# Hybrid decoder step on one core: the LayerNorm shift as extra token columns, the last expert's transposes inside the preceding down projection, and two groups of loads moved

## What is computed

```python
def layer_norm(x, g, b):
    mu = x.mean(-1, keepdims=True)
    var = jnp.square(x - mu).mean(-1, keepdims=True)
    return (x - mu) * lax.rsqrt(var + LN_EPS) * g + b

def moe(x, ...):                       # w_gate, w_up (16,1024,512), w_down (16,512,1024)
    for e in range(N_EXPERTS):
        h = jax.nn.silu(xt @ w_gate[e]) * (xt @ w_up[e])
        y = y + combine[:, e:e + 1] * (h @ w_down[e])

def rglru_mixer(x, conv_hist, h0, w_in, conv_w, conv_b, ...):   # layer 1
    y_br, x_br = jnp.split(x @ w_in, 2, axis=-1)                # w_in (1024, 2048)
    y_br = jax.nn.gelu(y_br, approximate=True)
    xc, conv_new = causal_conv(x_br, conv_hist, conv_w, conv_b)
    ...                                                         # gates, scan, output projection

x = layer_norm(ALPHA * x + f, ln_ffn_g[0], ln_ffn_b[0])          # end of layer 0, feeds layer 1
```

## Time and profile before

| | |
|---|---|
| median of three runs | 1479.97 us |
| profiled execution | 1482.55 us, of which the span in the profile is 1480.8 us |
| PE busy | 1265.6 us (85%) |
| DVE busy | 980.4 us (66%) |
| ACT busy | 721.2 us (49%) |
| POOL busy | 205.6 us (14%) |
| mean granted TensorE clock | 0.899 of full |
| last down projection of layer 0 ends | 811.1 us after the span's start |
| first projection of layer 1 starts | 864.1 us |
| `c_w_out` is issued; the output projection that needs it starts | 969.1 us; 1040.0 us |
| last down projection of layer 1 ends | 1437.0 us |

### The profile page before, as it was taken

One profiled execution on the slowest core, in us unless ns is written; L12 is line 12 of the kernel. 1 busy time (PEld: TensorE's weight loads), 2 busy tenths in 40 slices (PEclk: granted clock), 3 DMA queues, 4 the chain that ended last, 5 costly groups with the idle time before them and its releaser, 6 DMA issues.

```text
span 1480.8 us, 18030 instructions
## 1 busy us (share of the span) xinstructions
PE 1265.6 (85%) x6469; PEld 1015.8 (69%) x6469; DVE 980.4 (66%) x1462; ACT 721.2 (49%) x988; POOL 205.6 (14%) x265
## 2 busy tenths in 40 slices
PE   4999978888899489999998279987994899999970
PEld 4989877776345378888886179953453788888850
DVE  2766345442334589999995543738445999999957
ACT  2533222212001288888884542255012888888843
POOL 3111342211200110000000200136001100000002
PEclk9999989987599599999999579998995999999995
DMA  6121060001332579999982912020425799999825
GB/s 194 58 66 49 1 211 1 1 1 50 111 145 100 206 279 410 409 415 408 421 351 100 312 47 86 1 114 0 174 107 199 289 398 419 414 412 415 345 100 191
DMA packets 63103, 296.60 MB, mean 200 GB/s; under 512 B 6625, under 2 KB 32970, under 8 KB 50753
## 3 DMA queue, kind: packets, MB, share of 16 engines
q1 hardware_dynamic: 51136, 252.78, 44.2%
q0 software_dynamic: 7296, 26.22, 4.8%
q10 hardware_dynamic: 4608, 16.78, 2.9%
HBM read 268.87 MB, written 26.89 MB: 200 GB/s over the span
## 4 chain that ended last, share of the span: by engine, by line
PE 79%; DVE 10%; ACT 4%; issue 3%; POOL 2%; DMA 1%; SPq 0%; POOLq 0%; DVEq 0%; ACTq 0%
PE bank L1026 24%; PE bank L1056 12%; PE bank L950 6%; PE bank L612 4%; PE bank L613 4%; PE bank L640 4%; PE bank L641 4%; PE bank L937 3%; PE bank L1016 2%; PE bank L1152 2%; PE bank L961 1%; PE bank L599 1%; PE bank L1044 1%; PE bank L836 1%; PE bank L701 1%
## 5 line engine op out<-in xcount | busy, mean ns | idle before, releaser
L1178 ACT ACTIVATE GU_HIGH<-work 128x1024 fp32r<-128x1024 f32 x256 | 269.8, 1060 | 65.0 <-PE bank L1026 65.0
L1026 PE MATMUL bank<-GU_HIGH,XGT_HIGH 128*128 128x512 f32 x512 | 206.1, 402 | 13.3 <-DVE XGT_LOW_B L2084 13.3
L2108 DVE TENSOR_TENSOR WUP_LOW<-work,GU_HIGH 128x1024 fp32r<-128x1024 f32 x128 | 153.5, 1221 | 15.9 <-ACT GU_HIGH L1178 11.6
L2108 DVE TENSOR_TENSOR WGT_LOW<-work,GU_HIGH 128x1024 fp32r<-128x1024 f32 x128 | 155.3, 1222 | 12.0 <-ACT GU_HIGH L1178 4.0
L2115 DVE TENSOR_TENSOR WDN_LOW<-work,WDN_HIGH 128x1024 fp32r<-128x1024 f32 x128 | 151.7, 1221 | 7.8 <-ACT WDN_HIGH L1178 3.6
L1178 ACT ACTIVATE WDN_HIGH<-work 128x1024 fp32r<-128x1024 f32 x128 | 135.3, 1063 | 43.6 <-PE bank L1056 43.6
L1178 ACT ACTIVATE work<-bank 128x512 f32<-128x512 f32 (+4 forms) x148 | 59.5, 445 | 134.1 <-PE bank L694 29.5
L1026 PEld LDWEIGHTS bank<-GU_HIGH,XGT_HIGH 128*128 128x128 f32 x512 | 98.5, 192 | 34.0 <-DVE XGT_LOW_B L2084 14.5
L1178 ACT ACTIVATE W_HIGH<-work 128x1024 fp32r<-128x1024 f32 x36 | 38.0, 1059 | 150.2 <-PE bank L613 80.6
L1056 PE MATMUL bank<-WDN_HIGH,HT_HIGH 128*128 128x512 f32 x256 | 103.9, 406 | 2.8 <-DVE HT_LOW L2095 2.8
L1026 PE MATMUL bank<-GU_HIGH,XGT_LOW_A 128*128 128x512 f32 x256 | 102.8, 402 | 0.0
(11 more groups left out here) (457 smaller groups left out, 2924.1 us busy)
## 6 DMA issues: line engine op xcount, KB each, us to landing
work<-in_moe_w_gate_dram SPq DMA_DIRECT2D x32, 2048.0 KB
work<-in_moe_w_up_dram SPq DMA_DIRECT2D x32, 2048.0 KB, 10.0
work<-in_moe_w_down_dram SPq DMA_DIRECT2D x32, 2048.0 KB, 9.4
y_rows<-work ACTq DMA_DIRECT2D x32, 512.0 KB, 10.3
work<-in_ab_w_in_dram SPq DMA_DIRECT2D x10, 1024.0 KB, 5.6
work<-in_c_w_in_dram SPq DMA_DIRECT2D x8, 1024.0 KB, 9.1
x_rows<-X SPq DMA_DIRECT2D x8, 512.0 KB, 2.6
work<-in_c_w_out_dram SPq DMA_DIRECT2D x1, 4096.0 KB, 12.8
```

The source lines that it names most:

```text
L1026: last = mm(psum, x, w, start=(k == m == 0), stop=(k == KD - 1 and m == 2))
L1178: return nc.scalar.activation(out, in_, ACT.Copy, scale=scale)
L2108: V.tensor_tensor(low[u][:, 2 * n:2 * n + 2, :], w[u][:, 2 * n:2 * n + 2, :], high, ALU.subtract)\
```

## The change

- `last_downs` puts the four transposes of expert 15 between slices 1 and 2 of down(14), into bank 4. Their high and low parts go to `XGT_HIGH` and `XGT_LOW_A`, whose tokens are no longer needed. down(15) accumulates in banks 0 and 2 in place of 7 and 6. Both layers do this.
- In `norm(1)` the transposed tile is only multiplied by the gain; the bias is not added. The bias column becomes two extra token columns (the same column twice) of `XT_HIGH` and `XT_LOW`, now 578 columns wide. The matmuls of the second token half have 290 columns. Column 288 of each result is the weight matrix times the bias; ACT copies it to `in_shift[:, c]` and adds it as the bias of the Gelu, or of an Identity in place of a copy.
- `mixer1_rows` now also makes the two columns' high and low parts, takes a Sqrt of a constant on ACT, and rounds and splits the weight blocks 0 and 1; `norm(1)` no longer does.
- SP loads the first two blocks of `c_w_in` after down(14), ahead of the wait for down(15); before, they came after the gate matrices. The tables of layer 1's first norm are loaded after the projections, ahead of `c_w_out`.

```diff
+            def down_part(u, g, f, high, low, banks):
+                pe.wait_ge(down_split, 4 * g + (f + 1))
+                for half in (1, 0):
+                    cols = slice(512 * half, 512 * half + 512)
+                    for n, (x, w) in enumerate(((high, WDN_HIGH), (high, WDN_LOW[u]), (low, WDN_HIGH))):
+                        last = mm(bank[banks[half]][:, :], x[:, f, :], w[:, f, cols],
+                                  start=(f == n == 0), stop=(f == 3 and n == 2))
+                last.then_inc(down_used, 1)
+            def last_downs(g):
+                pe.wait_ge(ht_ready, g)
+                pe.wait_ge(y1_out, g - 1)
+                for f in (0, 1):
+                    down_part(0, g - 1, f, HT_HIGH, HT_LOW, (7, 6))
+                pe.wait_ge(h_ready, g + 1)
+                for f in range(4):
+                    last = tr(heads_of(4)[:, f, :], every(HB[1], FF // P, f), ident[:, :])
+                last.then_inc(h_ps, 1)
+                for f in (2, 3):
+                    down_part(0, g - 1, f, HT_HIGH, HT_LOW, (7, 6))
+                pe.wait_ge(ht_ready, g + 1)
+                for f in range(4):
+                    down_part(1, g, f, XGT_HIGH, XGT_LOW_A, (0, 2))
...
                 up(l, 8, 1, base + 15)
-                down(l, 0, base + 14)
-                h_transposed(1, base + 15)
-                down(l, 1, base + 15)
+                last_downs(base + 15)
...
+                if l == 0:
+                    sp.wait_ge(down_used, 4 * (base + NE - 1))
+                    for n in range(2):
+                        sp.dma_start(W0[n], c_w_in[0].rearrange("(k p) c -> p k c", p=P)[:, :, 256 * n:256 * n + 256])\
+                          .then_inc(w_in[n], 16)
                 sp.wait_ge(down_used, 4 * (base + NE))
...
-                lnp(0, 1, ln_mix_g, ln_mix_b)
                 sp.wait_ge(ysel_in[2], 32)
...
-                for n in range(8):
+                for n in range(2, 8):
...
                 sp.wait_ge(proj_ps, NPROJ + 16)
+                lnp(0, 1, ln_mix_g, ln_mix_b)
                 sp.dma_start(WO1, c_w_out[0].rearrange("(k p) d -> p k d", p=P)).then_inc(wo_in, 16)
...
-                        last = mm(bank[(3, 6, 7)[c % 3]][:, 0:TH], w[:, k, :], x[:, k, TH:T], **ends)
+                        last = mm(bank[(3, 6, 7)[c % 3]][:, 0:TH + 2], w[:, k, :], x[:, k, TH:T + 2], **ends)
...
-                            last = nc.scalar.activation(XT[:, k, tile_cols(t)], heads_of(TILE_BANK(t) + 1, P, ROWS[t])[:, k - 4, :],
-                                                        ACT.Identity, bias=ffn_col[:, 1, k:k + 1], scale=ffn_col[:, 0, k:k + 1])
+                            last = copy(XT[:, k, tile_cols(t)], heads_of(TILE_BANK(t) + 1, P, ROWS[t])[:, k - 4, :],
+                                        ffn_col[:, 0, k:k + 1])
...
-                        for k in range(4):
-                            last = V.tensor_scalar(XT[:, k, tile_cols(t)], heads_of(TILE_BANK(t), P, ROWS[t])[:, k, :],
-                                                   ffn_col[:, 0, k:k + 1], ffn_col[:, 1, k:k + 1], ALU.mult, ALU.add)
-                        last.then_inc(xt_lo, 1)
+                        V.tensor_tensor(XT[:, 0:4, tile_cols(t)], heads_of(TILE_BANK(t), P, ROWS[t]),
+                                        ffn_col[:, 0, 0:4].unsqueeze(2).broadcast_to([P, 4, ROWS[t]]), ALU.mult).then_inc(xt_lo, 1)
...
+                g = base + 15
+                round_units("up", 8, 1, g)
+                store(1, g - 2, 13)
+                h_rounded(g - 1)
+                silu(1, g)
+                round_down(8, 1, g, (0, 1))
+                act.wait_ge(h_ps, g + 1)
+                copy(XGT_HIGH[:, 0:4, :], heads_of(4)).then_inc(ht_high, 1)
+                round_down(8, 1, g, (2, 3))
+                result(8, 0, g - 1)
+                store(0, g - 1, 14)
+                result(8, 1, g, 0)
+                store(1, g, 15)
...
+                act.wait_ge(hist_out, 3 + 3)
+                rounded.end(copy(XT_HIGH[:, :, T:T + 2], ffn_col[:, 1, :].unsqueeze(2).broadcast_to([P, KD, 2])), 0, "b")
+                nc.scalar.activation(norm_eps[:, 1:2], norm_eps[:, 0:1], ACT.Sqrt)
+                round_w(0)
+                round_w(1)
...
+                    shift = in_shift[:, c:c + 1]
+                    copy(shift, sbk[:, TH:TH + 1]).then_inc(shift_out, 1)
+                    act.wait_ge(shift_out, c + 1)
...
+                        for to, part in ((buf[:, CONV - 1:CONV - 1 + TH], pb[:, 0:TH]), (buf[:, CONV - 1 + TH:EXT_P], sbk[:, 0:TP - TH]),
+                                         (ext_samples(buf)[:, :, CONV - 1:], sbk[:, TP - TH:TH].rearrange("p (s l) -> p s l", s=NS))):
+                            last = nc.scalar.activation(to, part, ACT.Identity, bias=shift)
...
+                split_units("up", 1, g)
+                h_split(g - 1)
+                h_product(1, g)
+                split_down(1, g, (0, 1))
+                dve.wait_ge(ht_high, g + 1)
+                V.tensor_tensor(XGT_LOW_A[:, :, :], heads_of(4), XGT_HIGH[:, 0:4, :].bitcast(F32), ALU.subtract).then_inc(ht_ready, 1)
+                split_down(1, g, (2, 3))
+                result(8, 0, g - 1)
+                result(8, 1, g, 2)
...
+                rounded.wait(dve, 0, "b")
+                dve.wait_ge(y_stored[0], arrivals(0, 8))
+                split.end(V.tensor_tensor(XT_LOW[:, :, T:T + 2], ffn_col[:, 1, :].unsqueeze(2).broadcast_to([P, KD, 2]),
+                                          XT_HIGH[:, :, T:T + 2].bitcast(F32), ALU.subtract), 0, "b")
+                split_w(0)
+                split_w(1)
```

More of the change, by code:

```diff
@@ L220, in hybrid_trunk @@
         GI = view(26112, (KD, T))
-        EXT1 = [work[:, 30720 + EXT * s:30720 + EXT * (s + 1)] for s in range(3)]
-        TMP = view(32529, (2, T))
+        EXT1 = [work[:, 30752 + EXT * s:30752 + EXT * (s + 1)] for s in range(3)]
+        TMP = view(32561, (2, T))
         lhistT = view(33681, (KD, 24))
@@ L1051, in down @@
                 for f in range(4):
-                    pe.wait_ge(down_split, 4 * g + (f + 1))
-                    for half in (1, 0):
-                        cols = slice(512 * half, 512 * half + 512)
-                        for n, (x, w) in enumerate(((HT_HIGH, WDN_HIGH), (HT_HIGH, WDN_LOW[u]), (HT_LOW, WDN_HIGH))):
-                            last = mm(bank[7 - half][:, :], x[:, f, :], w[:, f, cols],
-                                      start=(f == n == 0), stop=(f == 3 and n == 2))
-                    last.then_inc(down_used, 1)
+                    down_part(u, g, f, HT_HIGH, HT_LOW, (7, 6))
+            def last_downs(g):
[12 more added lines that the diff above has]
+                    down_part(1, g, f, XGT_HIGH, XGT_LOW_A, (0, 2))
             def experts(l):
@@ L1368, in root @@
                         act.wait_ge(norm_stats, q * NT + t + 1)
-                        nc.scalar.activation(lnw[0:r, t, 14:15], lnw[0:r, t, 13:14], ACT.Sqrt, bias=norm_eps[0:r, :],
+                        nc.scalar.activation(lnw[0:r, t, 14:15], lnw[0:r, t, 13:14], ACT.Sqrt, bias=norm_eps[0:r, 0:1],
                                              scale=1.0 / D).then_inc(norm_root, 1)
@@ L1391, in norm @@
                 root(0)
-                for t in range(NT + 3):
+                for t in range(NT + 2):
                     if t + 1 < NT:
@@ L1454, in store, with step @@
                        .then_inc(y_stored[u], 16)
-                def step(i, v, before, more=True):
+                def step(i, v, before):
                     u, g = (1 + v) % 2, i * 2 + (base + 1 + v)
@@ L2109, in split_units, with split_down @@
                             .then_inc(gu_split, 1)
-                def split_down(u, g):
-                    for f in range(4):
+                def split_down(u, g, some=range(4)):
+                    for f in some:
                         dve.wait_ge(down_rounded, 4 * g + (f + 1))
```

80 lines of the change are left out of this document (31 added, 49 removed).

## The result

The changed kernel takes 1472.43 us at the median of four runs (1470.24 to 1473.53), the kernel before 1480.11 in four runs beside it (1479.16 to 1480.52). The ratio is 0.9947, with a 95% interval of 0.993 to 0.9964: 7.7 us less. The profiled execution took 1473.53, with a span of 1471.6 against 1480.8 before; its mean granted clock is 0.905 against 0.899.

The account below looks back on a forecast made before the run. PE was taken as the bound (79% of the chain). Terms -6.2 + 2.9 - 3.15 + 0.3 + 0.5 - 3.5 = -9.15 us gave 1470.8 from the 1479.97 median, put at 1471.0; range 1466.5 to 1476.

Parts of the forecast that it names:

- the tail in one piece at full clock: Sign: down(14), transposes and down(15) as one PE run of 11.4 to 11.8 us at full clock, both layers.
- the first sum behind block 1's split: Sign in layer 0's norm: DVE's first sum right behind the split of weight block 1, not behind a gather.
- 6.4 us a projection: Sign: projections take 6.4 us each as before; one longer than 6.5 us would be wrong.
- the gates 1.4 us after the last: Sign: PE starts the gates about 1.4 us after the last projection.
- The tails: End of the experts: closing PE's gap between down(14) and down(15) gives -6.2 us in layer 0, -3.5 in layer 1.
- Between the experts and the sums: Layer 0: new ACT and DVE work on bias columns, Sqrt and two weight blocks delays the first sum, +2.9 us.
- The table load: Early Sqrt's load, 1.28 us plus 0.2, counted ahead of layer 0's sums; its removal from the norm given nothing.
- The norm: Layer 0, first sum to first projection: one DVE step, shorter activations and no block 0 at the end, -3.15 us.
- The columns: Projections: 384 matmuls of the second token half have two more columns, +0.3 us at 2.4 GHz.
- the last eviction: ACT's extra column copy and bias pointers, hidden in all projections but the last before the gates, +0.5 us.
- rival 3: Projections: wider token arrays read more slowly; 12 ns more per matmul cancels the gain; 1490 or above, chance 0.06.
- Rival 2: Layer 0: weight block loads hold up expert 15's store, so the sums start 3.4 us later; 1474.4, chance 0.15.

Follow-up runs that it names:

- the tails alone: Kernel before with only the new order of the last two down projections; norm, bias and all loads as before: 1469.71 us, ratio 0.9931.
- the rest alone: Changed kernel's edits except the tails, with down(14), transposes and down(15) in the old order: 1481.91 us, ratio 1.0015 against the kernel before.
- The kernel without the early load: Changed kernel without the Sqrt of a constant ahead of the weight blocks, so its table load falls back into the norm: 1470.96 us, ratio 0.9942.
- the tails with the pitch: Tails alone, but with the two token arrays 578 columns apart per k slice in place of 576: 1471.8 us, ratio 0.9945.
- the load late: Changed kernel with the first two weight blocks loaded after expert 15's store has landed, preparation still ahead of the sums: 1471.91 us, ratio 0.9944.
- the kernel with the preparation in the loop: Changed kernel with rounding and splitting of weight blocks 0 and 1 moved into the norm's loop, early loads kept: 1471.38 us, ratio 0.9944.

## Why the prediction was right, and where it was not

1471.0 was forecast, 1472.43 measured, 1.4 us above it. All signs that the prediction named came out: the tail in one piece at full clock, the first sum behind block 1's split, 36 us of norm, 6.4 us a projection, the gates 1.4 us after the last.

**The tails: right in mechanism and size.** -6.2 was forecast for layer 0 and -6.35 measured, -3.5 and -3.6 for layer 1. Down(14), transposes and down(15) take 11.45 us in a piece; I had 11.57 with an allowance of 0.2 for late operands, of which nothing shows. The experiment with the tails alone gives the whole gain. Restarting down(15) cost 0.3 us in layer 1 (5.76 against 5.45), which the two numbers include.

**Half of the tail's gain in layer 0 is clock, and there the forecast had luck.** I took 3 us of half level as fixed for layer 0 and absent for layer 1, because one profile showed it so. The profile of the rest alone shows it in both layers with the same code, so layer 1 could have gained 2.5 us more. No profile shows layer 0 without it. The timed 9.6 us of the tails alone (8.4 to 12.1 by the interval) fits one fall in the kernel before, as an average; none would give about 6.9 and two about 12.5, an estimate from the segments.

**Between the experts and the sums: the step was right, the size was off.** +2.9 forecast, +3.6 measured. DVE's first sum stands behind block 1 and not behind a gather, as the prediction said. The work itself took a little less: the first sum starts 2.6 us later than with the tails alone when the small loads are undisturbed (16.54 against 13.98). The term that was missing is the issue and landing of the nine small loads behind two 1 MB blocks, 1.0 us. I had written that they "move with it"; what moves past a queue's other work has to be costed again.

**The table load: I gave its removal from the norm nothing, which holds.** The kernel without the early load has a norm 0.16 us longer, hardly more than one profile can tell. Ahead of the sums it costs 1.6 us, of which I had counted 1.5. The Trainium skill's 2.66 us for a switch of tables ("ScalarE: Activation LUTs", section "What ACT_TABLE_LOAD costs") is not what this case shows: the load at 815.71 takes 1.28 and the next root follows it by 0.01 us, and taking load and root away gives 1.6 us in all.

**The norm: -3.15 forecast, -3.5 measured.** All kernels with the norm's part show 35.6 to 36.9 us against 38.9 to 39.1. No run splits this into its three edits, but the two timelines place the terms. The four activations of tile 0 to `XT`, before and in the changed kernel:

```profile
836.56 1.48 ACT L1189 ACTIVATE XT<-bank,ffn_col 128x128 f32<-128x128 f32 x4
```

```profile
831.70 1.12 ACT L1202 ACTIVATE XT<-bank,ffn_col 128x128 f32<-128x128 f32 x4
```

They take 0.36 us less where I had 0.3. DVE's step takes 0.69 in place of 1.37, and from tile 0's step to tile 1's it is 3.65 us in place of 4.33: -0.68, as forecast (-0.7), once. The three later steps each follow 0.36 sooner, and the short tile's four activations take 0.37 less: -1.46 together, forecast -1.15. The end, without block 0, gives -1.2 (-1.3), and 0.2 comes ahead of tile 0's step, which I had not counted.

**The columns and the last eviction.** Eviction +0.5 forecast, +0.47 measured. The matmuls +0.3 forecast, +0.67 measured: +1.0 at the full clock for the pitch against before, -0.3 because the clock rose three matmuls earlier. The columns themselves, the term that I had priced, cost next to nothing. The miss is rival 3 in small. I had said that it needs 12 ns a matmul to turn the result; it is 1.0 to 1.3.

**The layer 1 stretches.** I forecast nothing for the 452 us between the first gate and the last experts. The changed kernel took 0.9 more there, the others with the norm's part 0.3 to 1.4 more, the tails alone 0.4 less, the tails with the pitch 0.75 more. The changed kernel's repetition shows 0.9 again, so scatter between executions is not the likely cause. In all eleven profiles with the kernel's normal flow the difference arises in the first 205 us; over the rest, in layer 1's experts, they agree within 0.02 us. Nothing in that stretch was tested; its cause is open.

**Rival 2** had the mechanism right, its size too large and the consequence wrong. The store of expert 15 is held up by the weight blocks: it takes 6.11 us to land and 3.25 with the load late, and the first gather starts 8.99 us after the tail in place of 6.13. The rival took the store at 10.1 us and had the gather at 817.7, which is 12.8 after the tail; the delay is 2.85 us and not 6.7. And the first sum stood behind the splits, so none of it reached the end; the kernel with the preparation in the loop shows it in the open, with a wait of 2.95 us. My count of the bytes still in flight gave "some 2 us" (by its own numbers, 799.4 + 7.5 - 805.6, it is 1.3). The estimate by the Trainium skill's rule ("DMA: Bandwidth & Descriptors", section "Queues, rings and completion order") was nearer 1 us and hidden: hidden it was, but too small by 2 us.

**The sum.** By segment: tails -9.95 (forecast -9.7), before the sums +3.6 (+2.9), norm -3.5 (-3.15), projections +1.1 (+0.8): -8.75 in place of -9.15. Untouched stretches add -0.5 in this pair of profiles, which brings it back to -9.25; that the two cancel is luck. So nearly all of the 1.4 us lies in the executions: the profiled execution of before was 2.4 us above the median of its four runs, that of the changed kernel 1.1 above, so the medians differ by 7.7 us and not by 9.

## What to carry to other kernels

An idle stretch of PE at the end of a loop is worth its length (3.8 us here) and, in some executions, nearly as much again in clock (3.1 us); where a free bank lets the next operand's transposes run inside the matmuls before, both go. Work taken out of a loop in which two engines wait for each other gained nothing here by being put ahead of the loop's first input: look for the waits inside the loop, and take the place where the engine that does it stands idle. And an early load was paid by the store and the small loads that followed it (2.9 and 1.0 us); if such a cost seems absent, look what covers it, for the next improvement will uncover it.

## What the runs showed of the hardware that I had not expected

- With the pitch between the k slices of the token arrays (and the places of the buffers behind them) the pace of TensorE changes a little: fp32r matmuls of 288 columns come every 132.9 to 133.2 ns at 2304 bytes, 134.2 at 2312. At 2368 bytes and 288/290 columns it is 133.7.
- The same gap of 3.8 us before the same 24 matmuls was followed by a granted clock of 0.65 (8.5 us) in one layer and by full speed or nearly so (5.76 us) in the other, and in another kernel with the same code there by 0.69 (8.3 us).
- The projections' first matmuls run at a granted clock of 0.50, and their number differed between the executions from 12 to 25, at 0.107 us each.
- A 0.5 MB store issued 6.3 us after two 1 MB loads (803.77 and 797.48) took 6.11 us to land in place of 3.25 without them (first gather 8.99 against 6.13 us after the tail).
